# Stick-breaking attention by a running product along the keys in place of log-space prefix sums by matmul

## The reference, cut to what matters

```python
scale = 1.0 / math.sqrt(dh)                       # dh = 64
for i in range(T // SB_BLOCK):                    # blocks of 128 queries
    q0 = i * SB_BLOCK; kend = q0 + SB_BLOCK
    z = einsum('bhqd,bhkd->bhqk', q[:, :, q0:kend], k[:, :, :kend]) * scale
    mask = kpos[None, :] < qpos[:, None]          # strictly causal
    log_keep = where(mask, log_sigmoid(-z), 0.0)  # log(1 - beta), beta = sigmoid(z)
    suffix = cumsum(log_keep, axis=3, reverse=True) - log_keep
    weights = where(mask, exp(log_sigmoid(z) + suffix), 0.0)
    out = einsum('bhqk,bhkd->bhqd', weights, v[:, :, :kend])
```

## Time and profile before

| | us |
|---|---|
| Median of 3 runs | 4065.07 |
| Lowest and highest of them | 4060.56, 4078.79 |
| Span of the profiled execution, slowest core (core 4) | 4079.7 |
| Attention stage of the first sequence in it (895.5 to 1482.8) | 587.3 |
| Attention stage of the second sequence (2910.5 to 3498.0) | 587.5 |
| PE, ACT, DVE, POOL busy over the span | 3401.8, 1848.9, 1041.1, 900.0 |

### The profile page before, as it was taken

One profiled execution on the slowest core, in us unless ns is written; L12 is line 12 of the kernel. 1 busy time (PEld: TensorE's weight loads), 2 busy tenths in 40 slices (PEclk: granted clock), 3 DMA queues, 4 the chain that ended last, 5 costly groups with the idle time before them and its releaser, 6 DMA issues.

```text
span 4079.7 us, 48843 instructions; the slowest of 8 cores (4049.4 to 4079.7 us)
## 1 busy us (share of the span) xinstructions
PE 3401.8 (83%) x16119; PEld 1516.5 (37%) x16416; DVE 1041.1 (26%) x1473; ACT 1848.9 (45%) x3293; POOL 900.0 (22%) x1097
## 2 busy tenths in 40 slices
PE   5989999757777787999849799996577777889996
PEld 2334444323332333444314344442323323334442
DVE  3532111350110122222346322213501100221114
ACT  3313333308779745333233333333297778343331
POOL 0000000055446430000000000002564455100000
PEclk9879999879999998999969899998799999999997
DMA  5212222200000011222342122221000000112222
GB/s 125 31 21 37 39 37 39 36 13 3 6 6 1 6 16 26 38 38 39 67 139 34 24 39 39 39 38 28 16 1 6 6 4 4 21 29 39 39 37 93
DMA packets 69221, 133.02 MB, mean 33 GB/s; under 512 B 7664, under 2 KB 7664, under 8 KB 68336
## 3 DMA queue, kind: packets, MB, share of 16 engines
q0 software_dynamic: 50256, 94.69, 15.7%
q1 hardware_dynamic: 18720, 35.20, 2.7%
HBM read 207.75 MB, written 16.78 MB: 55 GB/s over the span
## 4 chain that ended last, share of the span: by engine, by line
PE 65%; ACT 18%; issue 9%; DVE 4%; DMA 2%; POOL 1%; ACTq 1%; SPq 0%; DVEq 0%; POOLq 0%
PE ps L404 61%; ACT ps L796 5%; ACT Wt_83 L810 4%; ACT Wt_84 L810 4%; ACT mix L449 3%; PE ps L788 2%; PE ps L724 1%; DVE xn L464 1%; DVE mix L669 1%; DMA oT<-rt_58 1%; DMA hT<-xT 1%; ACTq L126 1%; ACT ms L455 1%; DVE st_70 L634 0%; POOL st_70 L641 0%
## 5 line engine op out<-in xcount | busy, mean ns | idle before, releaser
L404 PE MATMUL ps<-xn,wring 128*128 128x512 bf16 x5768 | 1297.4, 384 | 25.4 <-DVE xn L464 11.1
L404 PE MATMUL ps<-mix,wring 128*128 128x512 bf16 x5018 | 1117.6, 383 | 5.6
L404 PEld LDWEIGHTS ps<-xn,wring 128*128 128x128 bf16 x5888 | 579.8, 99 | 738.8 <-issue 96.0
L385 POOL DMA_DIRECT2D wring<-wblk x344 | 181.9, 529 | 2637.3 <-PE ps L404 2609.5
L404 PEld LDWEIGHTS ps<-mix,wring 128*128 128x128 bf16 x5120 | 504.4, 99 | 616.2 <-issue 43.7
L507 DVE TENSOR_TENSOR hT<-ps,hT 128x512 f32<-128x512 f32 x512 | 354.2, 692 | 1397.6 <-PE ps L404 1393.5
L796 ACT ACTIVATE ps<-ps 128x512 f32<-128x512 f32 (+3 forms) x640 | 346.4, 541 | 133.1 <-PE ps L790 132.9
L449 ACT ACTIVATE mix<-hT 128x4096 bf16<-128x4096 f32 x40 | 144.2, 3604 | 474.8 <-PE ps L404 450.9
L404 PE MATMUL ps<-mix,cbs 128*128 128x512 bf16 x315 | 137.2, 610 | 250.5 <-ACT mix L449 249.6
L807 POOL TENSOR_TENSOR Cs_81<-Cs_81,Lp_79 128x512 bf16<-128x512 bf16 (+3 forms) x288 | 284.8, 989 | 221.8 <-ACT Lp_79 L798 100.6
L807 POOL TENSOR_TENSOR Cs_82<-Cs_82,Lp_80 128x512 bf16<-128x512 bf16 (+3 forms) x288 | 284.9, 989 | 169.2 <-ACT Lp_80 L798 83.7
(11 more groups left out here) (120 smaller groups left out, 2549.6 us busy)
## 6 DMA issues: line engine op xcount, KB each, us to landing
wring<-wblk POOLq DMA_DIRECT2D x344, 256.0 KB, 3.8
hT<-xT SPq DMA_DIRECT2D x64, 256.0 KB, 12.7
oT<-rt_58 SPq DMA_DIRECT2D x22, 256.0 KB, 2.5
oT<-rt_59 SPq DMA_DIRECT2D x22, 256.0 KB, 2.5
oT<-rt_60 SPq DMA_DIRECT2D x20, 256.0 KB, 2.5
wmv<-wmov POOLq DMA_DIRECT2D x4, 1024.0 KB, 9.2
cfs<-cf SPq DMA_DIRECT2D x1, 1088.0 KB, 7.2
sgst<-sg SPq DMA_DIRECT2D x1, 512.0 KB, 10.4
```

Source lines behind the costliest of these rows:

```text
L385: (lambda slot, b: (lambda e: e.dma_start(out=self.wring[:, slot, :], in_=self.wblk[b])))(slot, b),
L404: ins = pe.matmul(out_ap, lhsT=l, rhs=r, start=(first and i == 0), stop=(last and i == n - 1), **kw)
```

## The change

The attention is turned round: 128 queries lie on the partitions and up to 512 keys along the free dimension. An item covers both heads of a pair, one block of 128 queries and one chunk of up to 512 keys, from the chunk with the query's own position downwards: 40 items per pair.

- Two matmuls, one for each head on its own 64 partitions, give z for both heads in two PSUM banks; a mask matmul is added on the diagonal chunk.
- One ACT instruction turns both into 1 - beta = Sigmoid(-z/8), in place in PSUM.
- DVE sets the column at the right edge of `P` (1, or the left column of the chunk before) and runs one `tensor_tensor_scan` for each head from right to left: state = data0 * state + 0, the running product, into `P` in fp32.
- A subtraction of `P` from itself shifted by one column gives the weights in bf16 (`Wq`), on POOL in three items of four, on DVE in the fourth.
- The weights have queries on the partitions, and the product with v wants keys there. So SP issues one DMA transpose for the item, from `Wq` to `Wk`.
- Matmuls of v with `Wk`, 64 output partitions for each head, accumulate in one bank; ACT copies it to `mix` after each four query blocks.

The step of the subtraction follows one item behind, the value matmuls four items behind (`LAG = 4`). `P` and `Wq` have three buffers, `Wk` has five, z has three pairs of banks. The q, k, v projections of the next pair are cut into 12 groups (`qkv_groups`) spread among the items of the present pair, all through one bank (7) and evacuated by ACT; k and v have two buffers by pair, and q is written straight into the part of `mix` that the pair's output later takes. Only the first pair's projections stand ahead of the items. The zeroed second copies of q and v, their POOL memsets, `Lp`, `Cs`, `Wt` and the two summing matrices are gone.

```diff
         for a in range(4):
-            for which in (0, 1):
-                slot, Lr = self.next_block()
...
+            gemm.append(self.qkv_groups(a))
+        for f in gemm[0]:
+            f()
...
+            items = self.att_items(a)
+            todo = gemm[a + 1] if a < 3 else []
+            done = 0
+            for n, (z, w, av) in enumerate(items):
+                z()
+                self.pend_w.append(w)
+                self.pend_av.append(av)
+                if len(self.pend_w) > 1:
+                    self.pend_w.pop(0)()
+                while done < len(todo) and done * len(items) < (n + 1) * len(todo):
+                    todo[done]()
+                    done += 1
+                if len(self.pend_av) > LAG:
+                    self.pend_av.pop(0)()
...
+                    S.op("act", lambda e: e.activation(out=z3, in_=z3, func=AF.Sigmoid, scale=-0.125),
+                         reads=L_z, writes=L_z)
+                    if first:
+                        S.op("dve", lambda e: e.memset(P[:, :, 512:513], 1.0), writes=[L_P])
+                    else:
+                        S.op("dve", lambda e: e.tensor_copy(out=P[:, :, 512:513], in_=pv[0][:, :, pv[2]:pv[2] + 1]),
+                             reads=[pv[1]], writes=[L_P])
...
+                        S.op("dve", lambda e, h=h: e.tensor_tensor_scan(
+                            out=P[:, h, o:512][:, ::-1], data0=zt[:, h * 512:h * 512 + w][:, ::-1],
+                            data1=self.zeros[:, 0:w], initial=1.0 if first else pv[0][:, h, pv[2]:pv[2] + 1],
+                            op0=ALU.mult, op1=ALU.add),
+                             reads=[self.L_zeros] + ([] if first else [pv[1]]), writes=[L_P, L_z[h]])
...
+                    eng = "dve" if n % 4 == 3 else "pool"
+                    S.op(eng, lambda e: e.tensor_tensor(
+                        out=Wq[:, 0:2 * w].rearrange("p (h n) -> p h n", h=2), in0=P[:, :, o + 1:513],
+                        in1=P[:, :, o:512], op=ALU.subtract), reads=[L_P], writes=[L_Wq])
+                    S.op("sp", lambda e: e.dma_start_transpose(out=Wk[:, 0:w // 64, :], in_=Wq[:, 0:2 * w]),
+                         reads=[L_Wq], writes=[L_Wk], dma_key=("wk", n % NWT))
...
+                                ins = pe.matmul(av[h * 64:(h + 1) * 64, qc], lhsT=Va[:, c * 4 + j, h * 64:(h + 1) * 64],
+                                                rhs=Wk[:, h * nb + j, :], start=(first and j == 0),
+                                                stop=(c == 0 and j == nb - 1), skip_group_check=True)
```

More of the change, by code:

```diff
@@ L17 @@
 RING = 5
+NP = 3
+NW = 3
+NWT = 5
+LAG = 4
 NEG = -30000.0
@@ L329, in _alloc_fixed @@
[L329 to L349, removed]
+        self.kT = []
+        self.Va = []
@@ new lines, in _alloc_fixed @@
+        for i in range(2):
+            t, o = self.sb("kT%d" % i, [128, SEQ], BF16, off=o)
+            self.kT.append(t)
+            t, o = self.sb("Va%d" % i, [128, 16, 128], BF16, off=o)
+            self.Va.append(t)
+        self.P = []
+        self.Wq = []
+        self.Wk = []
+        for i in range(NP):
+            t, o = self.sb("P%d" % i, [128, 2, 513], F32, off=o)
+            self.P.append(t)
+        for i in range(NW):
+            t, o = self.sb("Wq%d" % i, [128, 1024], BF16, off=o)
+            self.Wq.append(t)
@@ L350, in _alloc_fixed @@
+        for i in range(NWT):
+            t, o = self.sb("Wk%d" % i, [128, 8, 128], BF16, off=o)
+            self.Wk.append(t)
+        self.L_kT = [[LT("kT%d_%d" % (i, t)) for t in range(4)] for i in range(2)]
+        self.L_Va = [[LT("Va%d_%d" % (i, t)) for t in range(4)] for i in range(2)]
+        self.L_P = [LT("P%d" % i) for i in range(NP)]
+        self.L_Wq = [LT("Wq%d" % i) for i in range(NW)]
+        self.L_Wk = [LT("Wk%d" % i) for i in range(NWT)]
         self.scr_groups = {
@@ L423, in setup @@
         S.op("pool", lambda e: e.dma_start(out=self.cb[:], in_=self.cb_d), writes=[self.L_cb], dma_key="cb")
+        S.op("pool", lambda e: e.memset(self.zeros[:], 0.0), writes=[self.L_zeros])
         self.use_scratch("sgu")
@@ new lines, in layer1, with qkv_groups, f @@
+        for f in self.pend_w:
+            f()
+        for f in self.pend_av:
+            f()
+        self.bank_rr = 0
+        self.out_proj()
+        self.mlp(1)
+    def qkv_groups(self, a):
+        S = self.S
+        GB = 7
+        p = a % 2
+        out = []
+        for which in (0, 1):
+            st = {}
+            for t in range(4):
+                def f(which=which, t=t, st=st):
+                    if t == 0:
+                        st["s"] = self.next_block()
+                    slot, Lr = st["s"]
@@ L715, in layer1 @@
-                self.prefetch()
-            for n4 in range(4):
-                bi = gbank()
-                def fnv(pe, bi=bi, n4=n4, a=a):
+                        S.op("act", lambda e: e.activation(out=self.mix[:, 4 + a, ts], in_=self.bank_ap(GB), func=AF.Copy),
+                             reads=[self.L_bank[GB]], writes=[self.L_mix[4 + a][t]])
+                    else:
+                        S.op("act", lambda e: e.activation(out=self.kT[p][:, ts], in_=self.bank_ap(GB), func=AF.Copy),
+                             reads=[self.L_bank[GB]], writes=[self.L_kT[p][t]])
@@ L720, in fnv, with f @@
+                    if t == 3:
+                        self.prefetch()
+                out.append(f)
+        for n4 in range(4):
+            def f(n4=n4):
+                def fnv(pe):
                     ins = None
```

222 lines of the change are left out of this document (84 added, 138 removed).

## The result

| us | before | after |
|---|---|---|
| Median (lowest to highest) | 4071.6 (4060.6 to 4078.8) | 3976.5 (3972.3 to 3979.2) |
| Ratio after / before, 95% interval | | 0.9765 (0.9745 to 0.9786) |
| Span of the profiled execution | 4079.7 | 3974.5 |
| Attention stage, first and second sequence | 587.3, 587.5 | 538.0, 538.9 |

The forecast was 3978 us, with a stage of 544. In some executions of a program on all eight cores one die shows a lower granted clock and takes some per cent longer; the times given leave these out, but experiment 7 is read from the four cores of the other die, and the trace of experiment 2 is of such an execution. The two stages lose 49.3 + 48.6 = 98 us together, and the medians differ by 95: next to nothing else of the program moved.

The account below looks back on a forecast made before the run. DVE was taken to bound the attention: 160 items x 2.96 = 473, + 32 at the port + 39 head and tail = 544 us a sequence against 587; 4065 - 87 = 3978 us. Own range 3915 to 4077; with rivals, 3690 to 4300.

Parts of the forecast that it names:

- The bound: Attention items: DVE was taken as the new bound, at 2.96 us an item.
- the upper bound: Scan on DVE: 1.25 us for 512 columns, 1.09 for 435, against a lower bound of 0.61 for 435.
- The rival of one column a step: Scan on DVE: runs like the evacuations, DVE needs 2.00 us an item, 3673 us in all; chance 0.13.
- The port: Edge copy after a DVE subtraction: waits for POOL's subtraction, 32 us a sequence, bounds 0 and 81.
- The third rival: Edge copy waits for POOL's subtraction in three items of four: 4.5 us an item, 4402 us in all; chance 0.12.
- The transposes: One DMA transpose an item: taken as 2.5 us, hidden under DVE's 2.96.
- the rival's count of packets: Transposes set the pace: a packet per 256 bytes, 94 ns each, 5.1 us an item, about 4604 us; chance 0.18.
- The head: First pair's projections through one bank: 24 to 34 us a sequence, taken as 31.
- The tail: From the last scan to the output projection: about 8 us a sequence.
- The waits of DVE for itself: DVE instructions of an item each wait for the one before: 0.10 to 0.11 us each.
- the 87: Whole kernel: saving in us over both sequences, 43.5 each, taken from 4065.
- PE doesn't wait: Value matmuls: transposed weights are ready after 10.5 us, PE asks four items (12 us) later.

Follow-up runs that it names:

- experiment 7: Changed kernel with the value matmuls two items behind instead of four (`LAG = 2`): 4214.6 to 4220.4 us on four cores.
- experiment 2: Changed kernel with every transpose issued twice, the extra one into memory nobody reads: 3997.9 us in a single execution.
- experiment 1: Changed kernel with each scan replaced by a DVE multiply by one of the same width: 3713.7 to 3723.4 us, ratio 0.9143.
- Experiment 3: Changed kernel with all subtractions on POOL, none on DVE: 3866 to 3879 us, ratio 0.9518.
- 4: Changed kernel with all subtractions on DVE, none on POOL: 4102.0 to 4103.3 us, ratio 1.0096.
- experiment 6: Changed kernel with each subtraction queued straight behind its own scans instead of one item later: 3944.4 to 3958.2 us.
- experiment 10: Changed kernel with all subtractions on POOL, edge copies on ACT, heads and edge tracked separately, first projections alternating between two banks: 3698.8 to 3711.3 us, ratio 0.9115.
- experiment 9: Kernel before, old attention kept, with the next pair's projections spread among the present pair's items: 4010.9 and 4016.4 us, ratio 0.9868.

## Why the prediction was right

**The bound.** DVE paces the new items: confirmed by the 89%, by experiment 1 (take DVE's time away and the items follow) and by 3 and 4 (move subtractions off it or onto it).

**The scan.** It was not on any row, and the choice of the upper bound carried the forecast. The reason given for it, a chain within the column, fits what came. Its size was luck: the 1.25 us of the earlier trace rows belong to an instruction that takes 0.69 alone and waited for POOL, as the prediction itself says further down, and show no dear DVE instruction. The widths give 1283, 957, 690 and 424 ns at 512, 384, 256 and 128 columns (the first with a carried start): between 128 and 384 (957 - 424)/256 = 2.08 ns a column, twice the 1.04 of the earlier trace rows. The rival of one column a step is out. The Trainium skill, page "DVE: opcode table, instruction layouts, handler registers and perf-mode slots", section 6, puts the scan at half throughput; the 2.08 agree.

**The port.** 32 us were taken between bounds of 0 and 81, for a copy behind a DVE subtraction that finds POOL at work, in the 24 of 40 items that have a copy. 32.1 us were lost, in that very place (31 of 32 copies), and experiment 6 took the place away and the loss with it. The place and the mechanism were right; that the size fits to 0.1 us is luck, since 32 of the 40 subtractions have a copy behind them and not 24, at 0.98 us lost for each and not 1.33. The third rival, a wait in every item, fell on the reason given against it: behind a scan the copy starts 0.10 us ahead of POOL. Experiment 3 shows where that reason ends: POOL must not still be at the item before.

**The transposes.** Hidden, as forecast (experiment 2), and the rival's count of packets was right: 144,384 in 160 items are 902 an item, of 247 bytes. Its price was not: 40.0% of 16 engines for 501 us is 22 ns a packet, not 94, so 1.25 us an item and not 5.1. The Trainium skill, page "Advanced Engine Details and Errata", section "X-Bar Transpose (TRN2)", expects 350 to 400 GB/s; the 35.67 MB in 40.0% of 501 us are 178 GB/s, about half.

**What was off.** The head is 36.7 us, above its upper bound of 34: one bank that must be emptied between two groups costs 11 us against the 25.6 of experiment 10, where 7 had been counted. The tail is 3.9 instead of 8. POOL's subtraction takes 1.67 ns a column ((1892 - 611)/768), not 2.11. The waits of DVE for itself were counted 9 us too high: its idle time in the loop is 56.7 us, just the 57 of the sum, but records of neighbouring instructions overlap by 9. The terms of the sum nearly cancel, and leave the stages 6.0 and 5.1 us below the forecast. That 3978 and 3976.5 are so close is chance beyond that: the 87 were taken from 4065, and the median before is now 4071.6.

One step was right in its result and wrong as it was put: "PE doesn't wait". It does, 166.1 us in 97 waits for transposes in the first stage's loop (15 rows of the view of PE's waits, by buffers); the largest:

```profile
PE ps L827 <- DMA Wk_83<-Wq_82: 19.4, 8, 3.7
```

They cost nothing there, since the chain has 3.9 us to spare: DVE waits for z 1.5 us in that whole loop, and this is the largest of its rows:

```profile
DVE P_78 L806 <- ACT ps L798: 0.9, 3, 0.6
```

The chain was counted as 10.5 us up to the value matmuls and is 11.7 all round. The rival of the fast scan left it out: experiment 1, with multiplies of 0.69 us in place of the scans, came to 3719 and not to its 3673.

**What the forecast didn't say.** It priced old and new stage as wholes, and so never put the 3.08 us of two old items beside the new one's 2.96 + 0.2. That the whole gain would lie in the seams could have been read from its own terms.

Open is how much each part of experiment 10 gives by itself, and what held experiment 1 beside the chain.

## What to carry to other kernels

Split the time of an old loop into work and seams before costing a new one: here the rewrite was worth just the seams, by freeing the engine that the work between them needed, and over half of that came from moving this work alone (experiment 9). A loop that follows itself at a distance has two limits, its busiest engine and its chain of latencies divided by the items that the chain spans; when an engine is made faster, look at once at the other, and run the distance shorter to measure it. Where two engines share a port, order small instructions so that they start before the other engine's long one, or give them to a third engine.

## What the runs showed of the hardware

- A scan along the columns costs 2.08 ns a column on DVE, and a start carried from a tile 59 ns more than a constant (1283 against 1224 ns).
- An instruction of two columns that lies wholly in SBUF lasts up to 1.86 us instead of 0.17 when a POOL subtraction began before it, as a copy or as an addition; a scan that reads PSUM (1282 to 1285 ns in all 384 of its kind) and a memset (0.06 us) don't wait at all.
- A transpose of 128x1024 in bf16 from SBUF to SBUF takes SP 1.22 us to issue and lands after 3.1 us; its packets of 247 bytes take 22 ns, while the 1.9 KB ones of before took 94.
- The granted clock of TensorE fell in the new loop to a mean of 0.64 between its two levels, and to 0.50, the lower one (1.2 GHz), from 1300 to 1400 us, where PE does 35 of 100 us of work in short bursts; in experiment 9 it stayed at 0.97. The items of the changed kernel wait for DVE and not for PE, so this is no part of their 3.11 us.
